# Projecting a Fourier input from mirrored sums and differences, and moving a gate into the heads' projections

## The reference, cut to what matters

```python
i_in, z_f, z_b, q_in, gate_a, u_f, gate_f = split_proj(h @ w_in)
...
y_a = o.reshape(...) * jax.nn.silu(gate_a)          # o: the heads' normed output
spec = jnp.fft.fftn(ug, axes=(1, 3), norm="ortho").real   # ug: u_f by group, over tokens and channels
y = einsum("blgc,gcd->blgd", spec, w_four) + b_four
y_f = y * jax.nn.silu(gate_f)
out = concatenate([y_a, y_f]) @ w_out
```

## Time and profile before

| | us |
|---|---|
| median of 3 runs | 2387.86 |
| lowest and highest | 2384.53, 2388.24 |
| span of the profiled execution, first to last instruction | 2377.7 |
| PE busy / DVE busy / ACT busy in it | 2282.0 / 1453.0 / 502.9 |
| front, from the first fill after the transposes to the heads' first matmul | 116.1 to 601.7 |
| heads | 601.7 to 1809.5 |
| Fourier part of the tail | 1809.5 to 1994.2 |
| output part of the tail | 1994.2 to 2377.7 |

### The profile page before, as it was taken

How to read it: one execution, slowest core, us unless ns; L and a number is a source line. 1 busy time by engine, 2 the same in 40 slices (tenths; PEclk the granted TensorE clock), 3 DMA queues, 4 the chain that set the end, 5 groups by cost and what they waited for, 6 DMA issues and landing times.

```text
span 2377.7 us, 50649 instructions
## 1 busy us (share of the span) xinstructions
PE 2282.0 (96%) x22032; PEld 1940.2 (82%) x22032; DVE 1453.0 (61%) x3035; ACT 502.9 (21%) x785; POOL 44.0 (2%) x64
## 2 busy tenths in 40 slices
PE   7899999999999999999999999999997889999997
PEld 2799999988888888787888887877876777888886
DVE  4831111222677777776777777788888886665554
ACT  3611111111111112111111121111113334221221
POOL 0000000000000000000000000000000001000000
PEclk9999999999999999999999999999998999999999
DMA  7422223323333332323333323233425247433441
GB/s 285 155 89 74 78 87 96 95 79 109 99 99 116 97 117 92 121 83 117 99 119 98 112 92 121 88 125 112 123 64 200 111 180 277 167 143 145 172 164 53
DMA packets 215694, 288.64 MB, mean 121 GB/s; under 512 B 13610, under 2 KB 146866, under 8 KB 212146
## 3 DMA queue, kind: packets, MB, share of 16 engines
q1 hardware_dynamic: 128114, 172.28, 21.8%
q10 hardware_dynamic: 79728, 85.34, 10.3%
q0 software_dynamic: 7632, 27.79, 3.7%
HBM read 192.03 MB, written 93.33 MB: 120 GB/s over the span
## 4 chain that ended last, share of the span: by engine, by line
PE 87%; DVE 7%; DMA 3%; issue 1%; ACT 1%; SPq 1%; ACTq 0%; DVEq 0%
PE all_bank L61 25%; PE all_bank L63 23%; PE all_bank L62 23%; PE all_bank L1150 2%; PE all_bank L1151 2%; PE all_bank L1142 2%; PE all_bank L1096 2%; PE all_bank L1112 2%; PE all_bank L1125 1%; PE all_bank L1135 1%; DVE hidden_h_lo L369 1%; DMA tail_u<-piece_wave 1%; DMA head_query<-piece_query 1%; PE all_bank L744 1%; PE all_bank L727 1%
## 5 line engine op out<-in xcount | busy, mean ns | idle before, releaser
L61 PE MATMUL all_bank<-hidden_h_hi,head_hi 128*128 128x512 f32 x1184 | 492.4, 416 | 0.1
L63 PE MATMUL all_bank<-hidden_h_hi,head_lo 128*128 128x512 f32 x1184 | 466.6, 394 | 0.0
L62 PE MATMUL all_bank<-hidden_h_lo,head_hi 128*128 128x512 f32 x1184 | 464.4, 392 | 0.0
L61 PE MATMUL all_bank<-front_hi,hidden_h_hi 128*128 128x256 f32 x1024 | 291.9, 285 | 6.7 <-DVE hidden_h_lo L369 6.7
L62 PE MATMUL all_bank<-front_lo,hidden_h_hi 128*128 128x256 f32 x1024 | 288.5, 282 | 0.0
L63 PE MATMUL all_bank<-front_hi,hidden_h_lo 128*128 128x256 f32 x1024 | 288.5, 282 | 0.0
L1187 ACT ACTIVATE head_projected<-all_bank 128x512 f32<-128x512 f32 x148 | 88.4, 597 | 877.6 <-PE all_bank L63 877.6
L63 PEld LDWEIGHTS all_bank<-hidden_h_hi,head_lo 128*128 128x128 f32 x1184 | 223.3, 189 | 51.9
L61 PEld LDWEIGHTS all_bank<-hidden_h_hi,head_hi 128*128 128x128 f32 x1184 | 223.8, 189 | 45.2
L62 PEld LDWEIGHTS all_bank<-hidden_h_lo,head_hi 128*128 128x128 f32 x1184 | 224.2, 189 | 40.1 <-issue 0.3
L61 PEld LDWEIGHTS all_bank<-front_hi,hidden_h_hi 128*128 128x128 f32 x1024 | 197.5, 193 | 11.8 <-DVE hidden_h_lo L369 9.7
(11 more groups left out here) (232 smaller groups left out, 4063.4 us busy)
## 6 DMA issues: line engine op xcount, KB each, us to landing
head_raw<-in_w_in POOLq DMA_DIRECT2D x37, 512.0 KB, 4.9
head_value<-value_rows SPq DMA_DIRECT2D x64, 256.0 KB, 5.1
head_query<-piece_query SPq DMA_DIRECT2D x64, 256.0 KB, 6.6
head_out<-head_o ACTq DMA_DIRECT2D x64, 256.0 KB, 5.6
tail_o<-head_out SPq DMA_DIRECT2D x32, 512.0 KB, 5.4
front_raw<-in_w_in SPq DMA_DIRECT2D x17, 512.0 KB, 5.0
front_w_mod<-in_w_ada SPq DMA_DIRECT2D x8, 1024.0 KB, 13.9
front_stage<-in_x SPq DMA_DIRECT2D x16, 512.0 KB, 8.4
```

The source lines that it names most:

```text
L61: nc.tensor.matmul(out, st_hi, mv_hi, start=start, stop=False)
L62: nc.tensor.matmul(out, st_hi, mv_lo, start=False, stop=False)
L63: return nc.tensor.matmul(out, st_lo, mv_hi, start=False, stop=stop)
```

## The change

Front: the gate's 32 fills go. In their place u_f is projected, from tokens that are already folded. `pair_tokens(i)` (VectorE, 16 times) adds `h_hi` and `h_lo` and makes sums and differences of mirrored tokens, 512 columns each, which POOL stores to DRAM (`tokens`). `fold_wave_weights(k)` makes sums and differences of mirrored weight columns c and 256-c, so 128 instead of 256 columns a group. `wave_step(s)` multiplies them: 24 even steps (three turns of 342 token columns, eight k each; 12 matmuls for four groups and two narrow ones for column 128, `ps_mid`) and 16 odd steps (two turns of 512 columns). Tokens are loaded again from DRAM into four slots and split for each step. Results go to `waves_even`, `waves_odd`, `waves_mid`; POOL folds the latter. Three of four value blocks come first, the fourth last; the context's work is spread anew, and all four `residual_gate`s stand among the first head's units. Heads: the piece `wave` becomes `gate_a`, channels first, with Silu. Tail: tokens come folded once, in two buffers and half the channels, so `fold_once` goes and folds and splits have half the width; `channel_weights` makes 128 columns instead of 256, `channels` contracts over one block of 128 and adds one matmul for the middle channel in the even halves; the heads' gate is applied after the turn (`gate_heads`), from channels-first rows, and the last tile has buffers of its own (`a_set`). The scratch for POOL's DMA descriptors is cut to 4 KB, which gives a slab `spare` of 12 KB.

```diff
-    "wave": (COL_U, ACT.Copy, 1.0),
+    "gate_a": (COL_GA, ACT.Silu, 1.0),
 }
 OF_NEXT = ("query", "key_f", "key_b")
-OF_THIS = ("gate_f", "wave")
...
+    EVENS, ODDS = 3, 2
+    EVEN_N, ODD_N = (HALF + 2) // EVENS, HALF // ODDS
+    E_STEPS, STEPS = EVENS * KT, (EVENS + ODDS) * KT
+    FILLS = [*((0, f) for f in range(KT + 1)), (1, KT), *((1, f) for f in range(KT)), (2, KT), (2, 0), (3, KT), *((2, f) for f in range(1, KT))]
+    WAVE_FILL = len(FILLS)
+    FIRST_FILL = WAVE_FILL + (EVENS + ODDS) * FG
     UNITS = 3 * NG
-
...
+        for i in range(PAIRS):
+            at, k = i // KT * GRP, i % KT
+            pool.wait_ge(paired, i + 1)
+            pool.dma_start(tokens[0][k * P:(k + 1) * P, at:at + GRP], both[i % 2][:]).then_inc(pair_stored[i % 2], DMA)
+            pool.dma_start(tokens[1][k * P:(k + 1) * P, at:at + GRP], here[i % 2][:]).then_inc(pair_stored[i % 2], DMA)
+        for i in range(2):
+            pool.wait_ge(pair_stored[i], PAIRS * DMA)
+        pool.wait_ge(mid_stored, EVENS * DMA)
...
+        def load_wave_weights(k):
+            if k >= 2:
+                sp.wait_ge(w_low_done, k - 1)
+            sp.dma_start(w_raw[k % 2][:].rearrange("p g c -> p (g c)"), w_in[0][k * P:(k + 1) * P, COL_U:COL_U + FW]).then_inc(w_raw_here[k % 2], DMA)
+
+        def load_tokens(s):
+            odd, j, k = step_of(s)
+            at, n = j * (ODD_N if odd else EVEN_N), loaded_columns(s)
+            if s in (2, 3):
+                sp.wait_ge(product, fill_of(2, KT - 1) + 1)
+            if s >= 4:
+                wait_step(sp, s - 4)
+            sp.dma_start(slot(s)[1][:, 0:n], tokens[odd][k * P:(k + 1) * P, at:at + n]).then_inc(token_here[s % 4], DMA)
...
+        sp.wait_ge(z_done, HEADS)
+        for i in range(2):
+            sp.wait_ge(pair_stored[i], PAIRS * DMA)
+        for s in range(STEPS):
+            if s < KT:
+                load_wave_weights(s)
+            load_tokens(s)
+            if s == E_STEPS + KT + 3:
+                sp.wait_ge(w_low_done, 2 * KT)
+                load_forget(0, BLOCK_F)
...
+        def pair_tokens(i):
+
+            b, g, k = i % 2, i // KT, i % KT
+            wait_count(v, pair_stored[b], i // 2 * 2 * DMA)
+            wait_count(v, paired, i)
+            nc.vector.tensor_tensor(here[b][:], h_hi[g][:, k, :].bitcast(F32), h_lo[g][:, k, :].bitcast(F32), ALU.add)
+            if g:
+                nc.vector.tensor_tensor(there[:, GRP:GRP + 1], h_hi[3][:, k, 0:1].bitcast(F32), h_lo[3][:, k, 0:1].bitcast(F32), ALU.add)
+            nc.vector.tensor_tensor(there[:, 0:GRP], h_hi[3 - g][:, k, :].bitcast(F32), h_lo[3 - g][:, k, :].bitcast(F32),
+                                    ALU.add).then_inc(summed, 1)
+            v.wait_ge(summed, i + 1)
+            if i == 0:
+                v.wait_ge(row_set, 1)
+            nc.vector.tensor_tensor(both[b][:], here[b][:], there[:, GRP:0:-1], ALU.add)
...
+        def fold_wave_weights(k):
+            v.wait_ge(w_raw_here[k % 2], (k // 2 + 1) * DMA)
+            if k == 4:
+                v.wait_ge(s_done, HEADS)
+                v.wait_ge(product, fill_of(2, KT - 1) + 1)
+            if k == KT - 1:
+                v.wait_ge(s_out, HEADS * 2 * DMA)
+            left, right = w_raw[k % 2][:, :, 1:P], w_raw[k % 2][:, :, 2 * P - 1:P:-1]
+            nc.vector.tensor_copy(w_fold[k][:, :, 0:1], w_raw[k % 2][:, :, 0:1])
+            nc.vector.tensor_copy(w_odd[k][:, :, 0:1], w_raw[k % 2][:, :, 0:1])
+            nc.vector.tensor_tensor(w_odd[k][:, :, 1:P], left, right, ALU.subtract)
+            nc.vector.tensor_tensor(w_fold[k][:, :, 1:P], left, right, ALU.add).then_inc(w_folded, 1)
+
+        def wave_weights_low(k):
+            v.wait_ge(w_high_done, k + 1)
+            nc.vector.tensor_tensor(w_mid[:, k, FG:2 * FG], w_raw[k % 2][:, :, P], w_mid[:, k, 0:FG].bitcast(F32), ALU.subtract)
+            nc.vector.tensor_tensor(w_low[k][:], w_fold[k][:], w_high[k][:].bitcast(F32), ALU.subtract).then_inc(w_low_done, 1)
...
+        def tokens_low(s):
+            odd, j, k = step_of(s)
+            high, whole, low = slot(s)
+            n = loaded_columns(s)
+            v.wait_ge(token_high_done, s + 1)
+            if not odd and n < EVEN_N:
+                nc.vector.tensor_copy(high[:, n:EVEN_N], h_hi[2][:, k, 0:EVEN_N - n])
+                nc.vector.tensor_copy(low[:, n:EVEN_N], h_lo[2][:, k, 0:EVEN_N - n])
+            nc.vector.tensor_tensor(low[:, 0:n], whole[:, 0:n], high[:, 0:n].bitcast(F32), ALU.subtract).then_inc(token_low_done, 1)
...
+        for h in range(4, HEADS):
+            v.wait_ge(z_done, h)
+            split_block(block_c(h), 6 + 2 * h)
+            weigh(h - 1)
+            pair_tokens(2 * h)
+            pair_tokens(2 * h + 1)
+        v.wait_ge(z_done, HEADS)
         weigh(HEADS - 1)
-        v.wait_ge(z_done, HEADS - 1)
-        split_block(BLOCK_Q, 27, P)
-        weigh(0)
+        fold_wave_weights(0)
+        fold_wave_weights(1)
+        for s in range(E_STEPS):
+            if s < KT:
+                wave_weights_low(s)
+            tokens_low(s)
...
+        def evacuate_waves(turn):
+            odd = turn >= EVENS
+            j = turn - EVENS if odd else turn
+            size, rows_out = (ODD_N, waves_odd) if odd else (EVEN_N, waves_even)
+            for group in range(FG):
+                n_fill, n_store = WAVE_FILL + FG * turn + group, WAVE_STORE + FG * turn + group
+                o = n_store % 2
+                flat = out[o][:].rearrange("p u w -> p (u w)")[:, 0:size]
+                act.wait_ge(product, n_fill + 1)
+                act.wait_ge(stored[o], n_store // 2 * DMA)
+                nc.scalar.activation(flat, bank[n_fill % 4][:, 0:size], ACT.Copy).then_inc(evacuated, 1)
+                act.wait_ge(evacuated, n_fill + 1)
+                act.dma_start(rows_out[group * P:(group + 1) * P, j * size:(j + 1) * size], flat).then_inc(stored[o], DMA)
...
+        def wave_step(s):
+            odd, j, k = step_of(s)
+            size = ODD_N if odd else EVEN_N
+            high, whole, low = slot(s)
+            turn = EVENS + j if odd else j
+            if j == 0:
+                pe.wait_ge(w_low_done, KT + k + 1 if odd else k + 1)
+            pe.wait_ge(token_low_done, s + 1)
+            for group in range(FG):
+                n_fill = WAVE_FILL + FG * turn + group
+                if k == 0:
+                    pe.wait_ge(evacuated, n_fill - 3)
+                done = mm3(nc, bank[n_fill % 4][:, 0:size], w_high[k][:, group, :], w_low[k][:, group, :], high[:, 0:size], low[:, 0:size],
+                           k == 0, k == KT - 1)
+                if k == KT - 1:
+                    done.then_inc(product, 1)
+            if not odd:
+                if k == 0:
+                    pe.wait_ge(sig_done, HEADS)
+                    wait_count(pe, mid_copied, j)
+                nc.tensor.matmul(ps_mid, w_mid[:, k, :], high[:, 0:size], start=k == 0, stop=False)
+                done = nc.tensor.matmul(ps_mid[0:FG, :], w_mid[:, k, 0:FG], low[:, 0:size], start=False, stop=k == KT - 1)
+            if not odd or k < KT - 1:
+                done.then_inc(step_done, 1)
...
+        value_fill(2, KT - 2)
+        context_state(HEADS - 2)
+        value_fill(2, KT - 1)
         turn_key(HEADS - 1)
-        first_unit(block_c(0), 0, 2)
+        for s in range(2):
+            wave_step(s)
         context_state(HEADS - 1)
-        first_unit(block_c(0), 0, 3)
...
         def load_u(n):
-            pieces_stored(n)
-            sp.dma_start(u[:], wave[n * FC:(n + 1) * FC, :].rearrange("(c p) t -> p c t", p=P)).then_inc(u_here, DMA)
+            group = slice(n * P, (n + 1) * P)
+            sp.dma_start(u[0][n % 2][:], waves_even[group, 0:HALF + 1]).then_inc(u_here[n % 2], DMA)
...
-        def fold_once(n):
-            v.wait_ge(u_here, (n + 1) * DMA)
-            nc.vector.tensor_tensor(once[0][:, :, 1:HALF], u[:, :, 1:HALF], u[:, :, SEQ - 1:HALF:-1], ALU.add)
-            nc.vector.tensor_tensor(once[1][:, :, 1:HALF], u[:, :, 1:HALF], u[:, :, SEQ - 1:HALF:-1], ALU.subtract)
-            nc.vector.tensor_copy(once[0][:, :, 0:HALF + 1:HALF], u[:, :, 0:HALF + 1:HALF]).then_inc(once_done, 1)
-            v.wait_ge(once_done, n + 1)
...
+        def gate_heads(t):
+            v.wait_ge(turned, t + 1)
+            if t < NT - 1:
+                wait_count(v, a_used, t)
             for i in range(2):
                 ks = slice(i * KT // 2, (i + 1) * KT // 2)
-                last = nc.vector.tensor_tensor(a_lo[:, ks, :], ps_t[i], a_hi[:, ks, :].bitcast(F32), ALU.subtract)
-            last.then_inc(a_lo_done, 1)
+                last = nc.vector.tensor_tensor(a_raw[a_set(t)][:, ks, :], ps_t[i], ga[t % 2][:, ks, :], ALU.mult)
+            last.then_inc(gated, 1)
+
+        def split_heads_low(t):
...
-                for m in range(CC):
+                for half in (slice(0, P), slice(P, FC)):
+                    for k in range(CC):
```

(21 more changed lines are left out.)

624 lines of the change are left out of this document (398 added, 226 removed).

## The result

The changed kernel takes 2285.18 us (median of four runs, 2281.88 to 2287.57), the kernel before beside it 2386.2 (four runs, 2381.26 to 2388.24). The ratio is 0.9587, with a 95% interval of 0.9568 to 0.9606: 4.1% less time. The forecast was 2289 with a range of 2270 to 2322.

What follows compares the result with a forecast made beforehand. PE was taken to bound the kernel: only fewer matmuls help front and heads, waits count too in the tail. Front -58, heads 0, Fourier part -42, output part +1 give -99: 2387.9 to 2289 us, range 2270 to 2322.

Steps and rivals of the forecast that it cites:

- (1): Front, heads' context work: VectorE and PE both need 12.5 us a turn, so no loss; each further VectorE us costs one.
- (2): Front, weight fold: one load in flight, period 5.7 us against 2.15 of matmuls, six loads: +20 us, between +14 and +31.
- (3): Front, turns of the four banks: the third evacuation waits for the first one's store: +3.6 us, ends 2 and 8.
- (4): Front, token loads into four slots: hidden behind 4 x 2.15 us; costs only if landings pass 7 us.
- (5): Front, PE's clock: slower clock hidden while weights are late, afterwards costs one slow tail: +3 us, ends 0 and 6.
- (6): Front, POOL's folding of the middle row with its two loads, and the four residual_gates: all hidden.
- Tail, Fourier part: Tail: no fold_once, half-width folds and splits, fewer matmuls, tail_y waits gone: -42 us, ends -22.5 and -47.
- (A): Rival: transfers land late, weights in 5.0 us, stores in 3.5; weight fold +31, bank turns +8; 2304 us; chance 12%.
- (B): Rival: tail's waits stay, set by gate_y and copies, not folds; only the matmul count is won; 2309 us; chance 12%.
- (C): Rival: clock stays at 1.2 GHz through the wave steps; 34 steps take 83 us more; 2369 us; chance 6%.
- (D): Rival: pair stores on POOL's queue stall VectorE and PE in the heads' turns; slower than before, 2400 us; chance 3%.
- (E): Rival, better: weight landing 2.6 us, no clock loss, last waits gone; 2275 us; chance 9%.

Runs made afterwards that it cites:

- the experiment: Changed kernel plus three more 512-column VectorE additions in each of the four turns of heads 4 to 7: 2293.17 us, ratio 0.9617.
- the experiment with the added matmuls: Changed kernel plus fourteen matmuls of 342 columns into an unused bank after each of wave steps 1 to 5: 2289.23 us, ratio 0.9599.
- the last kernel: Changed kernel with weight buffers freed after the fold, four evacuation buffers, reordered tail work and loads ahead of the second store: 2254.11 us, ratio 0.9452.
- the folding experiment: Changed kernel plus eleven more 512-column VectorE operations in the folding of tail groups 1 to 3: 2308.05 us, ratio 0.9692.

## Why the prediction was right, and where its terms were off

The mechanisms of the two big terms, the front and the Fourier part, held. That the sum comes within 4 us is in part luck: the front lost 10 us more than forecast, and 7 of them came back in the heads and the start, where the forecast was 0.

**Heads, forecast 0, measured -4.4.** A change of the heads' length was one of the prediction's own signs that it is wrong, and it came. Work is the same (PE busy 1178.8 and 1178.1 us). The difference lies in PE's waits: those that the view calls "issue" (nothing in the profile ended them) add up to 16.7 us before and 11.0 after, at other places of the program; they are 17.8 in the second profile of the kernel before, and 6.1 to 11.9 in the eight others of the changed kernel and its variants, the fewest in the shortest stage (1200.2). Why, no run here tells; a change that leaves a stage's work alone can move it by this much.

**Front, matmuls, forecast -84.8.** Held: 2.18 us an even step against 2.15, 0.228 us a 512-column matmul against 0.230. The estimate by the Trainium skill (TensorE: Matmul & The Clock Gate, "Back-to-back issue gap"), 0.216 us for an isolated matmul of 512 columns, lies under the measured 0.228, so the rows were the better price.

**(1) Turns even, forecast 0.** Held, and shown by the experiment: no wait before the first wave step, a turn of 12.42 us on VectorE, and 7.6 us of loss for 8.7 added.

**(2) Weight chain, forecast +20.** Mechanism right and shown, though the waits bear the name `front_token_lo` and not `front_w_low`, as the prediction had it. The period was put at 5.7 us and is 5.86 (landing 3.7 where 3.5 was taken). The eight steps lost 23.1 us and wave step 0 waited 0.9 ahead of them, 4 over the forecast. Six periods of 5.86 less 2.17 are 22.1; the lead of 1 us that was subtracted was not there, and 1.1 is the lower clock, by the experiment with the added matmuls.

**(3) Bank turns, forecast +3.6.** The term that was off most by its size: 7.8 us, of which 7.4 are the waits for `front_out` and 0.4 those for `front_mid_out`, near the upper end of 8 that the prediction gave. The prediction let one evacuation a turn wait for a store. Two do, as ScalarE's timeline at the first turn shows; each ends a wait of PE of its own.

```profile
336.96 0.46 ACT L748 ACTIVATE front_out<-all_bank 128x342 f32<-128x342 f32 x1 [1.52 <-DMA waves_even<-front_out]
...
338.57 0.46 ACT L748 ACTIVATE front_out<-all_bank 128x342 f32<-128x342 f32 x1 [1.15 <-DMA waves_even<-front_out]
```

**(4) Tokens hidden** held: outside the weight phase no wait is for `front_token_lo`, and in the last kernel, whose weights are early, 2.4 us of such waits are left. **(5) The clock, +3**: 0.96 over the 42 us of steps 8 to 23 is 3.4 us at half speed, 1.7 lost; but the whole wave part was 3.7 us longer in another execution of the same program. There the waits differed too (9.3 us for `front_out`, 7.4 in the first). The size can't be said more closely. **(6) Hidden** held: no wait for POOL's folded middle row or a residual gate.

Together the front lost 36.8 us beside its matmuls (437.6 less 400.8) where 26.6 were forecast: 4.0 more in (2), 4.2 more in (3), 1.3 less in (5), and 3.3 that are spread over matmul prices and that no single row names.

**Tail, Fourier part, forecast -42, measured -40.7.** A middle group takes 33.97 us (forecast 33.3). The waits for `tail_y` vanished, and the folding put back brought 14.5 us of them again. The half clock behind a wait cost 1.5 us in one middle group of that experiment and about 3 in the other, where the difference of the earlier trace rows gave 2.8. What is left is what the prediction named, the halves behind `gate_y`, 1.64 us at the first of them in groups 1 and 2; in the last group it is 3.9, behind the splits of w_out. In the first group a wait of 3.1 us that nothing in the profile ends stands where the one for `tail_cw_lo` was.

**Tail, output part, forecast +1, measured +0.4.** At t = 1 PE waits 1.0 us for `tail_a_lo` (forecast 2.4), and the wait of 2.6 us for the last tile is gone. The wait of 3.7 us for `tail_f_lo`, tile 2's rows loaded behind three loads for the heads' rows, is nothing new. The kernel before had it too, 2.6 us long and with one of 0.85 ahead of it:

```profile
PE all_bank L61 <- DVE tail_f_lo L1754: 3.4, 2, 2.6
```

In the second profile of the kernel before it was 3.7 us. What lies behind PE's last matmul grew from 12.4 to 13.2 us.

**Around the span**, 10.2 us were left as they are; they are 1.9. It did no harm, since it cancels between the two kernels: the forecast takes a difference off the median.

**The rivals.** (A) fell: the landing is 3.7 to 3.8 us, not 5. Its price for the turns, 8, is what they cost, but with stores of the even turns in 2.6 us at the median and not 3.5: two waits a turn did it. (B) fell by the folding experiment. (C) fell: steps 8 to 39 took 90.6 us at clocks of 0.96 and 1.00; at half the clock their matmuls alone would take 157 (twice 16 x 2.18 + 16 x 2.74). The prediction's reading that the lower clock stands only behind waits of 3 us and more is wrong all the same: in the kernel before PE waits 2.6 us up to 2013.38, and from 2014.7 to 2018.0 the clock is 0.50; in the changed kernel it is 0.51 from 339.6 to 343.0, at the first turn, behind waits of 0.8 and 0.9 us. (D) fell: up to the weight phase no wait of VectorE is for a pair store (they land in 2.6 to 2.7 us at the median). (E) came nearest of the rivals, and not for its reasons: the weights and turns cost more than in it, and the heads less.

## What to carry to other kernels

Where an engine stands waiting for a load, ask what behind it in its list would release the next load: here the low half of a block, 0.7 us of work, stood behind a wait of 3.3 us and so kept the next load from starting, at 15 us in all. Evacuation through n buffers costs a wait for a store for every bank beyond n (here two of 0.8 to 1.2 us of PE at each even turn), not once a turn. When a step is moved on one engine, write down which transfers wait for it and what is queued behind these on the queue that issues them; the move that gained 5 us at its own place made the kernel 30 us slower through SP's queue, and gained again once the loads went ahead of the store.

## What was not expected of the hardware

- How long a weight load of 512 KB takes depends on how close it follows the one before. Behind it by 3.3 us or more it took 3.5 to 4.1 us over all profiles (once 4.6), by 2.7 to 2.9 us in the last kernel 4.5, 4.5 and 3.6 us (out at 297.25, 300.06 and 306.32), by 0.9 to 1.1 us 5.9 to 6.4 us (once 4.8). What else was in flight differs between these cases, so the reason stays open. The even flow is the fast one: 199 GB/s in the stretch with the low half early, 213 in the last kernel.
- The same program gets another clock in another execution: the Fourier part had 0.96 and 0.92 of the full clock and took 144.0 and 147.9 us, with PE idle for 15.4 and 14.4 us of it. The front took 437.6 and 441.1 us, there with other waits at the turns too. A difference of 4 us in one profile's stage proves nothing here, unless its waits show it.
- A heads stage with the same work is 1207.8 and 1209.2 us long in one program and 1200.2 to 1205.0 in the others, by waits that nothing in the profile ends.
